# Lighter VectorE work in the mixing stage, pre-added sums for four layer norms, and recurrence products over four quadrants

## The reference

```python
z = x @ w_in                      # 1024 -> 2120 columns, for three head groups
# A: an indexer scores the keys per query: sum over 8 heads of relu(iq . ik) * iw, causal;
#    the 256 best keys are kept; 6 query heads with rotary positions share one key/value head:
#    softmax over the kept keys, times v, then an RMS norm
# B: RWKV-7: a 64 x 64 state per head, decay, delta rule; 6 heads
# C: trailing means over 2/4/8/16 tokens minus the token, a small linear map
x = layer_norm(ALPHA * x + concat(A, B, C) @ w_out)
ffn = square(relu(x @ mlp_w1)) @ mlp_w2
ple = sigmoid(x @ pe_gate + b) * (p @ pe_proj)
x = layer_norm(ALPHA * x + ffn + ple)
```

## Time and profile before

| what | value |
|---|---|
| median of three runs | 3779.99 us (3774.95 to 3780.49) |
| the profiled execution's own time | 3774.45 us |
| its span, first to last instruction | 3772.6 us |
| TensorE busy | 3427.3 us (91%) |
| VectorE, ScalarE, POOL busy | 1784.7, 1068.7, 1121.2 us |
| mean granted TensorE clock | 0.954 |

### The profile page before, as it was taken

The page is one execution under the profiler, slowest core; times in us unless marked ns, Lnnn a source line. Parts: engine busy times, 40 slices in busy tenths (PEclk is TensorE's granted clock), DMA queues, the critical chain, the costliest instruction groups (busy, mean ns, idle before and its releaser), DMA issues.

```text
span 3772.6 us, 61018 instructions
## 1 busy us (share of the span) xinstructions
PE 3427.3 (91%) x23080; PEld 2462.0 (65%) x23080; DVE 1784.7 (47%) x3061; ACT 1068.7 (28%) x1875; POOL 1121.2 (30%) x940
## 2 busy tenths in 40 slices
PE   7889887898999999999988888779889999999997
PEld 3444444886667888888734445458765688888884
DVE  5689996344342222222348899844335122222224
ACT  3343224443122111122133432244412112122122
POOL 1274341651212222222114543335412222222221
PEclk9999998998999999999999998889999999999998
DMA  3100000000101111111111000000011111111111
GB/s 119 38 27 22 19 20 18 1 0 20 59 12 56 50 50 44 44 53 47 34 49 39 11 22 21 18 19 0 1 34 49 35 51 44 50 45 50 50 39 45
DMA packets 43864, 132.74 MB, mean 35 GB/s; under 512 B 9280, under 2 KB 11840, under 8 KB 43072
## 3 DMA queue, kind: packets, MB, share of 16 engines
q1 hardware_dynamic: 37280, 122.41, 10.0%
q10 hardware_dynamic: 6432, 8.40, 0.9%
HBM read 117.15 MB, written 5.24 MB: 32 GB/s over the span
## 4 chain that ended last, share of the span: by engine, by line
PE 59%; DVE 14%; DVEq 11%; issue 10%; ACT 2%; POOLq 2%; POOL 1%; ACTq 1%; DMA 0%; SPq 0%
PE bank L1021 14%; PE bank L1023 14%; PE bank L1022 14%; DVEq L1615 8%; DVE M L1611 8%; PE bank L751 3%; PE bank L629 2%; PE wide L601 2%; DVE PB L1627 2%; PE wide L751 1%; PE wide L606 1%; DVEq L1612 1%; DVE WK L1613 1%; PE bank L719 1%; POOLq L1503 1%
## 5 line engine op out<-in xcount | busy, mean ns | idle before, releaser
L1502 POOL TENSOR_TENSOR WL<-WR,WH 128x1024 fp32r<-128x1024 f32 x160 | 389.8, 2436 | 1492.0 <-ACT WH L1305 1491.3
L629 PE MATMUL bank<-X,WR 128*128 128x512 f32 x1088 | 532.2, 633 | 19.2 <-ACT A L1189 9.9
L1021 PE MATMUL bank<-XH,WH 128*128 128x512 f32 x1280 | 517.4, 404 | 19.8 <-DVE XL L1548 10.2
L1023 PE MATMUL bank<-XH,WL 128*128 128x512 f32 x1280 | 501.5, 392 | 0.0
L1022 PE MATMUL bank<-XL,WH 128*128 128x512 f32 x1280 | 501.5, 392 | 0.0
L1884 DVE TENSOR_TENSOR Y<-Y,bank 128x512 f32<-128x512 f32 x256 | 175.9, 687 | 492.1 <-PE bank L1023 492.1
L1021 PE MATMUL bank<-HH,WH 128*128 128x512 f32 x1024 | 400.4, 391 | 0.0
L1023 PE MATMUL bank<-HH,WL 128*128 128x512 f32 x1024 | 398.6, 389 | 0.0
L1022 PE MATMUL bank<-HL,WH 128*128 128x512 f32 x1024 | 398.4, 389 | 0.0
L629 PEld LDWEIGHTS bank<-X,WR 128*128 128x128 f32 x1088 | 206.0, 200 | 270.6 <-issue 243.8
L1305 ACT ACTIVATE WH<-WR 128x1024 fp32r<-128x1024 f32 x160 | 168.2, 1053 | 736.3 <-PE bank L1023 727.7
(11 more groups left out here) (275 smaller groups left out, 5141.7 us busy)
## 6 DMA issues: line engine op xcount, KB each, us to landing
WR<-in_w SPq DMA_DIRECT2D x128, 512.0 KB, 3.5
WR<-in_w_in SPq DMA_DIRECT2D x34, 512.0 KB, 3.5
WR<-in_w_out SPq DMA_DIRECT2D x16, 512.0 KB, 3.5
WR<-in_w_gate SPq DMA_DIRECT2D x16, 512.0 KB, 5.8
Y<-in_xT SPq DMA_DIRECT2D x2, 2048.0 KB, 13.1
out_T<-X SPq DMA_DIRECT2D x1, 4096.0 KB, 11.8
QZS<-QZ ACTq DMA_DIRECT2D x48, 64.0 KB, 2.0
QZS<-QZ ACTq DMA_DIRECT2D x64, 48.0 KB, 2.0
```

The lines of the kernel that those rows point to most:

```text
L629: mm = e.matmul(BK_[hf], WR[:, i % RING, kt, :], X[:, kt, hs(hf)], start=kt == 0, stop=kt == KT - 1)
L1021: e.matmul(BK_[b], WH[:, s, w, :], high[:, kt, q], start=kt == 0, stop=False)
L1023: mm = e.matmul(BK_[b], WL[:, s, w, :], high[:, kt, q], start=False, stop=kt == kts - 1)
L1502: e.tensor_tensor(WL[:, s, :, :], WR[:, i % RING, :, :], WH[:, s, :, :].bitcast(F32), ALU.subtract)
```

## The change

- **Mix, selection.** The last block in order, b = 2, has 384 columns. Its scores are copied negated and reversed, and 16 rounds take out the 128 that are to be dropped, in place of 32 for the 256 kept. Its mask takes one instruction, not two.
- **Mix, maximum.** `maximum` multiplies by -1/8 itself and keeps the minimum, written to NM; the small instruction behind it is gone.
- **Mix, rotation.** The product with the sine table is POOL's. VectorE does the cosine product as an item of its own (`iqc`, `qc`), later the sum.
- **Mix, orders.** All four lists are new.
- **Norms.** For the two norms of each layer, VectorE adds each finished tile of Y to a running sum (RB or RST), and the mean takes one matmul per half. In the MLP this is done in each of the eight rounds.
- **Recurrence.** The products of the even and the odd heads are issued together, so that neighbours in the queue use other rows and other columns of TensorE. `products` of the next tile stands ahead of `solved`, and both seed masks stand between VectorE's two copies of the state.

```diff
...
+DROPPED = -3e38
...
 VECTOR_ORDER = work_order("""
-    iq.3 z.2.0 q.0 vt.0 s.0.0 s.0.1 round.3*6 s.0.2 s.0.3 round.3*2 iq.4 round.3*4 s.0.4 s.0.5 q.1 z.2.1 inv.0
...
-    round.6*3 s.5.4 s.5.5 q.6 inv.5 round.6*4 fin.5 round.6*7 round.7*4 s.6.0 s.6.1 round.7*6 s.6.2 s.6.3 round.7*7
-    s.6.4 s.6.5 q.7 inv.6 round.7*3 fin.6 round.7*12 round.2*6 s.7.0 s.7.1 round.2*9 s.7.2 s.7.3 round.2*10 s.7.4
-    s.7.5 q.2 round.2 inv.7 round.2*6 fin.7 bias.2 s.2.0 s.2.1 norm.3 norm.4 norm.5 s.2.2 s.2.3 norm.0 norm.1 s.2.4
-    norm.7 s.2.5 norm.6 inv.2 fin.2 norm.2
+    iqc.3 iq.3 qc.0 q.0 z.2.0 vt.0 s.0.0 s.0.1 round.3*5 s.0.2 s.0.3 round.3*2 iqc.4 round.3*2 iq.4 round.3*3 s.0.4
...
+    qc.6 q.6 round.6 inv.5 round.6*2 fin.5 round.6*11 round.7*10 s.6.0 round.7 s.6.1 round.7*4 s.6.2 round.7 s.6.3
+    round.7*6 s.6.4 s.6.5 qc.7 q.7 round.7 inv.6 round.7*2 fin.6 round.7*7 round.2*5 s.7.0 s.7.1 round.2*7 s.7.2
+    s.7.3 round.2*4 bias.2 s.7.4 s.7.5 qc.2 q.2 inv.7 fin.7 s.2.0 s.2.1 s.2.2 s.2.3 norm.5 norm.0 norm.1 s.2.4 s.2.5
+    norm.6 inv.2 norm.7 fin.2 norm.3 norm.4 norm.2
 """)
 POOL_ORDER = work_order("""
-    lg.3.1 lg.3.2 lg.3.3 lg.3.4 lg.3.5 lg.3.6 lg.3.7 lg.4.1 lg.4.2 lg.4.3 lg.4.4 lg.4.5 lg.4.6 lg.4.7 bias.3
...
+    iq.3 q.0 q.1 lg.3.1 lg.3.2 lg.3.3 lg.3.4 lg.3.5 lg.3.6 lg.3.7 iq.4 iq.5 q.3 lg.4.1 lg.4.2 lg.4.3 lg.4.4 lg.4.5
+    lg.4.6 lg.4.7 bias.3 iq.6 lg.5.1 lg.5.2 lg.5.3 lg.5.4 q.4 shift.4*2 lg.5.5 lg.5.6 lg.5.7 shift.5*2 bias.4
...
 """)
...
-        MX = sb("MX", [P, NB, NH], m)
...
-        ln_sq_later = sem("ln_sq_later")
+        ln_sq_later, ln_sum = sem("ln_sq_later"), sem("ln_sum")
+        LN_SUMS = 2 + 2 * FB
...
+        sined = {"iq": sem("iq_sined"), "q": sem("q_sined")}
...
-            def layer_norm(u, landed=None):
+            def layer_norm(u, landed=None, sums=None, total=None):
-                    for kt in range(KT):
-                        mm = e.matmul(BK_[4 + hf], mean_ones, Y[:, kt, hs(hf)], start=kt == 0, stop=kt == KT - 1)
+                        for kt in range(KT):
+                            mm = e.matmul(BK_[4 + hf], mean_ones, Y[:, kt, hs(hf)], start=kt == 0, stop=kt == KT - 1)
+                    else:
+                        e.wait_ge(ln_sum, sums + (hf + 1))
+                        mm = e.matmul(BK_[4 + hf], mean_ones, total[:, hf, :], start=True, stop=True)
...
-            def products(T, g):
-
-                free(T, g, ("hE", "hO")[g])
+            def decayed(src, bank, col, h0, signals=False):
+
+                for turn in range(2):
+                    for g in range(2):
+                        c = g ^ turn
+                        mm = e.matmul(BK_[bank + g][chunk(c), col:col + 2 * CH], src[feats(g), h0 // 2, chunk(c)],
+                                      AR[feats(g), h0 // 2, :, chunk(c)], start=True, stop=True)
+                        if signals and turn:
+                            mm.then_inc(rb[bank + g].full, 1)
+
+            def products(T):
+
+                for g in range(2):
+                    free(T, g, ("hE", "hO")[g])
-                pair_products(BK_[g], 0, g)
-                pair_products(BK_[g], 4 * CH, g + 2).then_inc(rb[g].full, 1)
-
-            def pair_products(bank, col, h):
-
-                for j, src in enumerate((BT, KTL)):
-                    for c in range(2):
-                        mm = e.matmul(bank[chunk(c), col + 2 * CH * j:col + 2 * CH * (j + 1)],
-                                      src[feats(h), h // 2, chunk(c)], AR[feats(h), h // 2, :, chunk(c)],
-                                      start=True, stop=True)
-                return mm
-
-            def seed_products(T, g):
-
-                free(T, 2 + g, ("aE", "aO")[g])
+                decayed(BT, 0, 0, 0)
+                decayed(KTL, 0, 2 * CH, 0)
+                decayed(BT, 0, 4 * CH, 2)
+                decayed(KTL, 0, 6 * CH, 2, signals=True)
+
+            def seed_products(T):
+
+                for g in range(2):
+                    free(T, 2 + g, ("aE", "aO")[g])
-                pair_products(BK_[2 + g], 0, 4 + g)
+                decayed(BT, 2, 0, 4)
+                decayed(KTL, 2, 2 * CH, 4)
-                    for c in range(2):
-                        mm = e.matmul(BK_[2 + g][chunk(c), 4 * CH + CH * j:4 * CH + CH * (j + 1)],
-                                      AR[feats(g), j, 0, chunk(c)], BT[feats(g), j, chunk(c)],
-                                      start=True, stop=True)
-                mm.then_inc(rb[2 + g].full, 1)
+                    for turn in range(2):
+                        for g in range(2):
+                            c = g ^ turn
+                            mm = e.matmul(BK_[2 + g][chunk(c), 4 * CH + CH * j:4 * CH + CH * (j + 1)],
+                                          AR[feats(g), j, 0, chunk(c)], BT[feats(g), j, chunk(c)],
+                                          start=True, stop=True)
+                            if turn and j == 2:
+                                mm.then_inc(rb[2 + g].full, 1)
...
-                if more:
-                    products(T + 1, 0)
+                if more:
+                    products(T + 1)
-                if more:
-                    products(T + 1, 1)
-                    seed_products(T + 1, 0)
+                    seed_products(T + 1)
-                if more:
-                    seed_products(T + 1, 1)
...
-                for g in range(2):
-                    products(L * NB, g)
-                    seed_products(L * NB, g)
+                products(L * NB)
+                seed_products(L * NB)
...
-                for b in range(4):
-                    e.wait_ge(d_free[b], L * D_USES + (N_WOUT // 2 + 1))
-                layer_norm(L * 2 + 1)
+                layer_norm(L * 2 + 1, sums=L * LN_SUMS, total=RB)
...
-                for b in range(4):
-                    e.wait_ge(d_free[b], L * D_USES + (D_USES + 1))
-                layer_norm(L * 2 + 2)
+                layer_norm(L * 2 + 2, sums=L * LN_SUMS + 2 * FB, total=RST)
...
-                                 scale=HD ** -0.5, accum_out=SM[:, b, h:h + 1]).then_inc(probs_ready, 1)
+                                 scale=-1.0, accum_out=SM[:, b, h:h + 1]).then_inc(probs_ready, 1)
...
+                    elif kind in ("iq", "q"):
+                        k, n = ("iq", "q").index(kind), {"iq": 4, "q": 3}[kind]
+                        e.wait_ge(tables_landed, L * 32 + 32)
+                        e.wait_ge(swapped[kind], 64 * (rotations(L, (kind, b)) + 1))
+                        e.tensor_tensor(QZS[:, k, 0:n, :], QZS[:, k, 0:n, :], spread(ST[:, b * P:(b + 1) * P], n),
+                                        ALU.mult).then_inc(sined[kind], 1)
...
+            def add_to_sum(total, kt, hf):
+
+                if kt == 0:
+                    return
+                e.drain()
+                q = hs(hf)
+                ins = e.tensor_tensor(total[:, hf, :], Y[:, 0, q] if kt == 1 else total[:, hf, :], Y[:, kt, q], ALU.add)
+                if kt == KT - 1:
+                    ins.then_inc(ln_sum, 1)
+
...
-            def rotate(L, use, dst, n):
+            def rotate(L, use, dst, n, part):
-                if kind == "iq" and b != TOP_ORDER[0]:
+                if part == "cos" and kind == "iq" and b != TOP_ORDER[0]:
-                e.wait_ge(swapped[kind], 64 * (rotations(L, use) + 1))
-                e.tensor_tensor(dst[:, :, :], QZ[:, k, 0:n, :], spread(CT[:, q], n), ALU.mult)
-                e.tensor_tensor(QZS[:, k, 0:n, :], QZS[:, k, 0:n, :], spread(ST[:, q], n), ALU.mult)
-                e.drain()
+                if part == "cos":
+                    e.wait_ge(turned.free, turned.read(L, use))
+                    e.tensor_tensor(dst[:, :, :], QZ[:, k, 0:n, :], spread(CT[:, q], n), ALU.mult)
+                    e.drain()
+                    return
+                e.wait_ge(sined[kind], rotations(L, use) + 1)
-                src = work if i else SC[:, s, 0:n]
+                drop = b == TOP_ORDER[-1]
+                src = work if i or drop else SC[:, s, 0:n]
+                    if drop:
+                        e.tensor_scalar(work, SC[:, s, 0:n][:, ::-1], -1.0, None, ALU.mult)
+                        e.drain()
-                e.match_replace(work, M8[:, :], src, BIG)
-                if i < ROUNDS - 1:
+                e.match_replace(work, M8[:, :], src, DROPPED if drop else BIG)
+                if i < (ROUNDS // 2 if drop else ROUNDS) - 1:
...
-                bias = WK[:, SLOT[b], 0:n] if b else causal
+                bias = (SC if b == TOP_ORDER[-1] else WK)[:, SLOT[b], 0:n] if b else causal
-                e.tensor_tensor_reduce(out=PB[:, w, 0:n], in0=WIDE[w][:, 0:n], in1=bias, scale=1.0,
-                                       scalar=-3e38, op0=ALU.add, op1=ALU.max, accum_out=MX[:, b, h:h + 1])\
+                e.tensor_tensor_reduce(out=PB[:, w, 0:n], in0=WIDE[w][:, 0:n], in1=bias, scale=-HD ** -0.5,
```

(27 more changed lines are left out.)

79 lines of the change are left out of this document (39 added, 40 removed).

## The result

The changed kernel takes 3721.55 us (median; 3707.02 to 3730.42) beside 3779.55 us for the kernel before on the same chip: ratio 0.9846, 95% interval 0.9831 to 0.9861, 58 us less. Forecast were 102 us less, 3678, with a range of 3645 to 3720. The profiled execution is the quickest of the four, 3707.02 us (span 3705.2). All medians leave out one execution of e4 (3953.78 us) and one of e11 (5527.78 us), in which the mean granted clock was 0.83 and 0.55 and not 0.95.

The account below looks back on a forecast made before the run. VectorE was taken to set the mix, TensorE close behind, and TensorE the MLP. Mix -58, norms -47 and recurrence +3 gave -102 us: 3672.5 for the profiled execution, 3678 us as median, range 3645 to 3720.

Parts of the forecast that it names:

- Norms, -47: Four norms: pre-added sums bring the second root from 32.0 to 20.1 us, 47 us less in all.
- Added sums at nothing: Output projection and MLP: 126 added VectorE additions, 87 us, hidden behind TensorE and charged at nothing.
- Recurrence, +3: Recurrence: 0.5 us lost at each of 14 hand-overs, 4 us won at two loop starts; +3 us, bounds -26 and +14.
- Mix, -58: Mix: VectorE's savings less start and tail give 28.9 us per layer, 58 for two.
- Maximum, 7.4: Mix: 48 small VectorE instructions fewer save 7.4 us per layer, bounds 7.4 and 11.9.
- Rotation, 10.6: Mix: 14 sine products moved to POOL save VectorE 10.6 us net per layer, with no charge for contention.
- Selection, 21.3: Mix, last block: 16 rounds and one mask instruction fewer, one negating copy more; 21.3 us net per layer on VectorE.
- the tail at -8: End of the mix: fewer rounds between block 7's pairs of heads and in block 2's own; 8 us lost per layer.
- Start, -2.4: Start of the mix: `vt.0` behind two indexer products and POOL's slower sine product delay the first round 2.4 us.
- TensorE and the latencies hold the mix: Rival, mix: TensorE's idle time stays 65 us, not 49; 16 us lost per layer, 3710 us; chance 0.18.
- POOL holds the rotations: Rival, mix: each of 28 rotations' sums waits for POOL's sine product, 60 us back, 3738 us; chance 0.05.

Follow-up runs that it names:

- e4: Changed kernel with the last block selected as before: 32 rounds, two mask instructions, no negated copy; 3755.41 us, ratio 0.9937.
- e11: e8 with the sine products of the first three rotations back on VectorE; 3701.80 us, ratio 0.98.
- e1: Kernel before with only the pre-added sums for the four norms; 3734.16 us, ratio 0.9877.
- e5: Changed kernel with the recurrence of the kernel before, mix and norms as changed; 3717.09 us, ratio 0.9834.
- e12: Changed kernel with one more small VectorE instruction behind each of the 48 maxima; 3718.29 us, ratio 0.9844.
- e16: e15 with one more small VectorE instruction behind each of the 48 maxima; 3700.32 us, ratio 0.9776.
- e15: e8 run again on another chip, as base of its batch; 3695.99 us, ratio 0.9786.
- e14: e15 with all sine products back on VectorE; 3713.20 us, ratio 0.983.
- e17: Changed kernel with `vt.0` ahead of `lg.3.0` on TensorE, as before; 3717.40 us, ratio 0.9832.
- e8: e5 with earlier TensorE and ScalarE orders, VectorE's earlier order adapted, POOL's made by hand; lighter work kept; 3696.20 us, ratio 0.9786.
- e10: Changed kernel with 28 of 32 rounds in the five blocks before the last; 3658.06 us, ratio 0.969.
- e0: Changed kernel as it is, run and profiled again as base for other runs; 3721.68 us.
- e6: Changed kernel with the recurrence's second state copy between the two seed masks; 3719.93 us, ratio 0.985.
- e7: Changed kernel with each of a recurrence tile's 24 products of 128 columns issued twice; 3734.51 us, ratio 0.9892.
- e13: Changed kernel with three extra 128-column TensorE products ahead of each wait for probabilities; 3737.63 us, ratio 0.9888.
- e9: Changed kernel with one accumulation step of each input product left out, an eighth of each; 3714.42 us, ratio 0.9835.

## Why the prediction was wrong, step by step

- **Norms, -47: right.** 45 to 46.5 alone (e1), 20.3 us to the second root where 20.1 were forecast. As written, though, the steps of that sum (9.6, six of 1.45 and one of 0.87) end at 19.2.
- **Added sums at nothing: right.** From first norm to second it is 10.6 to 12.7 us less, about the norm's own gain.
- **Recurrence, +3: right in kind, perhaps too low.** +4.6 beside the changed mix, +11.6 alone, and the two can't be told apart. The hand-over of 0.5 us measured 0.43. The 4 us won at the starts of the loop did not come: the stage is entered 2 to 3 us sooner, and the first tile takes 3 to 4 us more. The slow tiles, 1.4 to 2.9 us each at a granted clock down to 0.63, were not foreseen.
- **Mix, -58: the failed step.** By medians the change has 17 us here (e5 against e1, 3717.1 against 3734.2), 8 to 9 per layer in place of 28.9. The sum took every microsecond off VectorE's list as one off the stage. Between the profiles of e1 and e5, from the first round to the end of the mix, VectorE's busy time falls by 25 to 26 us per layer (446.0 and 447.0 to 420.9), and its idle time grows by 15 to 17 (63.4 and 62.6 to 78.3 and 79.6). In the changed kernel's first profile, whose mix is the short one, VectorE is as busy and idle for 69.3. Its terms:
  - *Maximum, 7.4*: at most some 2 (e12, e16). Idle time of VectorE was taken for a list that never waits, but the maxima wait for scores. That a small instruction behind one is hidden by the wait ahead of the next is argued from those waits, not shown.
  - *Rotation, 10.6*: 8.6 in e15's order, 2.7 in the changed one. I had rows 5 and the rule of the Trainium skill (SBUF — State Buffer, "Who interferes with whom") and still charged nothing, on the argument that rounds fill most of VectorE's time. The share of the rounds was no cover: cosine products and sums took 18.8 us of layer 0's mix before, and 24.3 to 24.6 with the sine products on POOL and the changed order, 20.2 to 22.2 with the earlier ones. In the changed order seven cosine products take 1132 ns, in e15's 584.
  - *Selection, 21.3, with the tail at -8*: 17 (e4), where 13.3 would follow from both, and 11.3 with the 2.0 more that the held copy cost. So the tail cost less than was charged. In the earlier orders the rounds and the maximum together give only 10.5 per layer (e14 against e1). This step was sound, but its price hangs on the order.
  - *Start, -2.4*: 3.8 to 5.1 later than in the profile before, 1.1 to 3.3 later than in e1's, whose mix is the same as before. Of this 0.4 to 1.9 is `vt.0` (e17). Rows 6 show four instructions in 1.13 us, which are both products and not one; so by that row the place of `vt.0` was to cost 1.1 us and not 2.3.
  - *The orders themselves*: charged with start and tail alone, 10.4. With the lighter work kept and the orders taken back, 10.4 per layer come back (e5 against e8) although e8's last block has as few rounds. That part of the loss had no step in my sum; 2 to 3 us of it lie ahead of the first round and 4 in VectorE's busy time, 2.3 of them in the rotations.
- **The rivals.** "TensorE and the latencies hold the mix" named the right row: idle time of TensorE 68.3, not 49. But its reason fails: e10 shows that VectorE's rounds still set the pace. That its 3710 us lie nearest to the measured 3721.55 is luck in part: the 10 us per layer of the orders are not in it. "POOL holds the rotations" was right in part: VectorE's own instructions are held, while its waits on QZS stand at the start alone in the changed kernel. The price is the 10.6 us of the term less what the move gave, 2.0 to 7.9 us per layer and not 30.

**What stays open.** What in the order tables costs the other 8 us per layer, and which of the four lists; all four went back together in e8. It is not even a fixed price: the changed kernel's two profiles differ by 10 us per layer in the mix with the same lists, and in the first it is as short as e8's (539.4 and 542.2 beside 540.0 and 539.7). With the changed lists layer 0's mix took 539.4, 549.4, 549.3, 548.4 and 540.5 us (first profile, e0, e5, e6, e7), with the earlier ones and the same work 540.0 and 539.3 (e8, e15). Stretches of the same place, 370 to 415, first the slower execution and then the quicker one:

```profile
370.00:415.00 45.00, 42.94 (x161) 22.81 (x160) 35.09 (x51) 21.66 (x29) 21.74 (x14) 0.80 0.04 13
```

```profile
370.00:415.00 45.00, 39.05 (x199) 23.07 (x198) 39.82 (x59) 19.88 (x30) 21.02 (x14) 1.00 0.06 17
```

At a granted clock of 0.80 TensorE is busy 42.9 of 45 us with fewer matmuls, and VectorE does 35.1 us of work and not 39.8. That ties the loss to the clock in this place; it doesn't say what lowered the clock. e13 held it up with more work and won nothing. The profiles of e8 and e15 both show the shorter mix, and their runs mostly lie within 5 us of each other where the changed kernel's spread over 9 to 23.

## What to carry to other kernels

Read a new order of work as an edit of its own, and price it: here the same lighter work gave 8 to 9 us per layer in one order (e5 against e1) and 19 in another (e8 against e1). On an engine whose short instructions wait for another engine, count only the long runs of work that wait for nothing (the rounds paid 88% of their length, the small instructions behind the maxima nothing that could be measured). When work moves to GpSimd, look in the timeline for what VectorE starts while GpSimd is in the middle of an instruction, and put the two-input and copy forms elsewhere.

## What the runs showed of the hardware that was not expected

- A 128x384 negating copy on VectorE took 2.44 us behind a 2.35 us POOL instruction that had begun 0.12 us before it, and 2.09 us in e16, where it had begun 0.48 us before; in every profile that has it the copy ended 0.21 to 0.22 us behind POOL's instruction. Cosine products of 0.55 and 0.69 us took up to 1.68 and 2.19.
- With an eighth of the input products left out of the mix (e9), its granted clock was 0.89, where the full work had 0.93 and 0.90 in two executions, and the work that was left took 414 us where the full work had 425 and 437.
- The same program had a mix of 539 us in one execution and 549 in another, with granted clocks of 0.93 and 0.90 in it.
- In the recurrence the granted clock fell within a tile in some executions, and not in the same tiles.
